# Two transformer blocks on one core: whole x tiles first, a narrower wait at the second gated group, six projection groups by column blocks

## The reference, cut to what matters

```python
h = rmsnorm(x, norm_mix_g)
proj = h @ w_in            # 1024 x 15368
(ml_q, ml_k, ml_v, ml_o, ml_i, ml_f, sc_b, sc_c, sc_u,
 sb_q, sb_k, sb_v, g_ml, g_sc, g_sb) = split(proj)
y_ml = head_rmsnorm(sigmoid(ml_o) * mlstm(ml_q, ml_k, ml_v, ml_i + b_i, ml_f + b_f))
y_sc = short_conv(sc_b, sc_c, sc_u, conv_w)
y_sb = stick_breaking(sb_q, sb_k, sb_v)      # 16 heads of 64
merged = sigmoid(g_ml)*(y_ml @ w_ml_proj) + sigmoid(g_sc)*(y_sc @ w_sc_proj) + sigmoid(g_sb)*(y_sb @ w_sb_proj)
x = x + merged @ w_out
x = x + square(relu(rmsnorm(x) @ w_up)) @ w_down
x = rmsnorm(x, norm_final_g)
# second block
x = x + rms_norm(hybrid_mixer(rms_norm(x), ...) @ w_out_2)
h = rms_norm(x, pre_ffn_norm)
x = x + rms_norm((silu(h @ w_ffn_gate) * (h @ w_ffn_up)) @ w_ffn_down)
```

## Time and profile before

| | us |
|---|---|
| median of the timed runs (919.97, 922.23, 922.33) | 922.23 |
| the profiled execution's own time | 922.42 |
| its span in the trace | 920.7 |
| TensorE busy | 907.2 |
| VectorE busy | 591.8 |
| ScalarE busy | 489.7 |
| GpSimd busy | 45.4 |

### The profile page before, as it was taken

One profiled execution on the slowest core, in us unless ns is written; L12 is line 12 of the kernel. 1 busy time (PEld: TensorE's weight loads), 2 busy tenths in 40 slices (PEclk: granted clock), 3 DMA queues, 4 the chain that ended last, 5 costly groups with the idle time before them and its releaser, 6 DMA issues. The chain is left out here.

```text
span 920.7 us, 12881 instructions
## 1 busy us (share of the span) xinstructions
PE 907.2 (99%) x5334; PEld 791.6 (86%) x5334; DVE 591.8 (64%) x614; ACT 489.7 (53%) x573; POOL 45.4 (5%) x80
## 2 busy tenths in 40 slices
PE   8999999999999999999999999999999989999997
PEld 7998998789998888888888888889987878888886
DVE  4765656567887445556677755557795767777643
ACT  6434877883435443345555543446777755555441
POOL 3010111110010000000000000001000100000000
PEclk9999999999999999999999999999999999999999
DMA  7766444544255555555565565544832475555541
GB/s 251 235 245 227 157 142 136 181 137 132 98 184 183 186 196 205 191 190 201 179 185 186 191 207 194 183 140 144 277 136 92 139 227 184 183 183 206 203 163 46
DMA packets 99818, 163.93 MB, mean 178 GB/s; under 512 B 4896, under 2 KB 37507, under 8 KB 99632
## 3 DMA queue, kind: packets, MB, share of 16 engines
q1 hardware_dynamic: 99760, 163.11, 53.8%
HBM read 162.03 MB, written 3.16 MB: 179 GB/s over the span
## 5 line engine op out<-in xcount | busy, mean ns | idle before, releaser
L1504 DVE TENSOR_TENSOR wlo<-land,whi 128x2048 fp32r<-128x2048 f32 (+2 forms) x152 | 335.1, 2208 | 176.8 <-ACT whi L1077 175.8
L1077 ACT ACTIVATE whi<-land 128x2048 fp32r<-128x2048 f32 (+1 forms) x152 | 280.4, 1848 | 206.8 <-PE acc L546 145.5
L552 PE MATMUL acc<-xT,whi 128*128 128x256 f32 x528 | 152.1, 288 | 0.0
L554 PE MATMUL acc<-xT,whi 128*128 128x256 f32 x528 | 149.3, 283 | 0.0
L556 PE MATMUL acc<-xT,wlo 128*128 128x256 f32 x528 | 149.3, 283 | 0.0
L552 PEld LDWEIGHTS acc<-xT,whi 128*128 128x128 f32 x528 | 101.1, 192 | 2.9 <-issue 2.1
L554 PEld LDWEIGHTS acc<-xT,whi 128*128 128x128 f32 x528 | 101.2, 192 | 0.2
L556 PEld LDWEIGHTS acc<-xT,wlo 128*128 128x128 f32 x528 | 101.2, 192 | 0.0
L544 PE MATMUL acc<-whi,xT 128*128 128x512 f32 (+2 forms) x240 | 91.5, 381 | 0.0
L545 PE MATMUL acc<-wlo,xT 128*128 128x512 f32 (+2 forms) x240 | 90.3, 376 | 0.0
L546 PE MATMUL acc<-whi,xT 128*128 128x512 f32 (+2 forms) x240 | 90.1, 375 | 0.0
(11 more groups left out here) (401 smaller groups left out, 1374.5 us busy)
## 6 DMA issues: line engine op xcount, KB each, us to landing
land<-in_w_in SPq DMA_DIRECT2D x55, 1024.0 KB, 5.1
land<-in_w_up SPq DMA_DIRECT2D x16, 1024.0 KB, 5.3
land<-in_w_down SPq DMA_DIRECT2D x16, 1024.0 KB, 5.1
land<-in_w_ffn_gate SPq DMA_DIRECT2D x22, 512.0 KB, 4.0
land<-in_w_ffn_up SPq DMA_DIRECT2D x22, 512.0 KB, 5.1
land<-in_w_ffn_down SPq DMA_DIRECT2D x10, 1024.0 KB, 5.0
land<-in_w_in SPq DMA_DIRECT2D x14, 512.0 KB, 4.6
land<-in_w_out SPq DMA_DIRECT2D x6, 1024.0 KB, 5.1
```

Source lines behind the costliest of these rows:

```text
L552: mm(to, whi[:, s, k, cs], xh[:, k0 + k, :], start=first and c % 2 == 0, stop=False, skip_group_check=True)
L554: mm(to, whi[:, s, k, cs], xl[:, k0 + k, :], start=False, stop=False, skip_group_check=True)
L1077: activate(whi[:, u % PARTS, 0:m, 0:w], land[:, u % LANDS, 0:m, 0:w], ACT.Copy).then_inc(hi_ready, 1)
L1504: v.tensor_tensor(wlo[:, u % PARTS, 0:m, 0:w], land[:, u % LANDS, 0:m, 0:w], whi[:, u % PARTS, 0:m, 0:w].bitcast(F32), ALU.subtract).then_ ...
```

## The change

Three things. At the **front**, x comes as two whole token tiles, with one tile `lead` between them that holds the identity, the vectors already turned into columns, and the gate biases; the transpose of the vectors and its copy are gone, x is turned tile by tile, seven and four warm matmuls stand where nine and six did, ScalarE's table is loaded by a dummy instruction, the squares of x are taken after unit 2's split, and the spread of the norm's row moves from between units 1 and 2 into unit 2. The **second gated group** waits, ahead of its second pair of banks, for `gate2_ready` and `rest_out` in place of gu0's `read_dve`, and the first and the second pair each do their wlo matmuls right behind their whi matmuls (the same goes for up0). **Six groups** (sbk, mlq, mlk, two each) are done by blocks of 128 output columns: for each block four 512-column matmuls and four 256-column ones into a bank of its own, all four banks by one group; VectorE folds each bank with a reduction (`take_chunk`) and scales afterwards in SBUF. `SIDE` replaces `n % 2`: a group behind one by blocks starts on the same side.

```diff
+SIDE = [0]
+for _n in range(1, len(GROUPS)):
+    SIDE.append(SIDE[-1] if chunked(GROUPS[_n - 1][0]) else 1 - SIDE[-1])
...
     @block.sync
     def _(sp):
-        sp.dma_start(rows[0:V_ROWS, :], dram["vectors"]).then_inc(rows_in, 16)
-        sp.dma_start(con[:, 0:P], dram["con"][:, 0:P]).then_inc(con_in, 16)
...
+        for t in range(TT):
+            sp.dma_start(x_tok[:, t, :], dram["x"][t * P:(t + 1) * P, :]).then_inc(x_in[t], 16)
+            if t == 0:
+                sp.dma_start(lead[:, :], dram["lead"]).then_inc(lead_in, 16)
...
+        def chunk_product(u):
+            n, k0, m = UNITS[u]
+            name, _, _, kk, act, _ = GROUPS[n]
+            s = u % PARTS
+            wait_operand(name, act, k0 + m)
+            for c in range(NG // P):
+                to, cs = acc[:, (SIDE[n] + c // 2) % 2, c % 2, :], slice(c * P, (c + 1) * P)
+                if k0 == 0 and chunked(GROUPS[n - 1][0]):
+                    pe.wait_ge(chunk_read, chunks_before(GROUPS[n - 1][0]) + c + 1)
+                elif k0 == 0 and c == 0 and n >= 2:
+                    group_read(n - 2)
+                elif k0 == 0 and c == 2:
+                    group_read(n - 1)
+                if c == 0:
+                    pe.wait_ge(hi_ready, u + 1)
+                for k in range(m):
+                    mm(to, whi[:, s, k, cs], xT[:, k0 + k].rearrange("p a t -> p (a t)"), start=k0 + k == 0, stop=False,
+                       skip_group_check=True)
+                if c == 0:
+                    pe.wait_ge(lo_ready, u + 1)
+                for k in range(m):
+                    last = mm(to[:, 0:T], wlo[:, s, k, cs], xT_hi[:, k0 + k, :], start=False, stop=k0 + k == kk - 1,
+                              skip_group_check=True)
+                if u == LAST_U[name] and c < NG // P - 1:
+                    last.then_inc(chunk_done, 1)
+            last.then_inc(units_done, 1)
...
+            if k0 == 0 and n >= 1 and chunked(GROUPS[n - 1][0]):
+                pe.wait_ge(chunk_read, chunks_before(GROUPS[n - 1][0]) + 2)
+            elif k0 == 0 and n >= 2:
+                group_read(n - 2)
...
                 if pair is not pairs[0]:
-                    group_read(n - 1)
+                    if name == "gu1":
+                        pe.wait_ge(gate2_ready, 1)
+                        pe.wait_ge(rest_out, D_FF // NG + 1)
+                    else:
+                        group_read(n - 1)
...
-            pe.wait_ge(lo_ready, u + 1)
-            for k in range(m):
-                for c in range(NG // P):
-                    last = mm(to[:, c, 0:T], wlo[:, s, k, c * P:(c + 1) * P], xT_hi[:, k0 + k, :], start=False,
-                              stop=k0 + k == kk - 1, skip_group_check=True)
+                pe.wait_ge(lo_ready, u + 1)
+                for k in range(m):
+                    for c in pair:
+                        last = mm(to[:, c, 0:T], wlo[:, s, k, c * P:(c + 1) * P], xT_hi[:, k0 + k, :], start=False,
+                                  stop=k0 + k == kk - 1, skip_group_check=True)
...
-            if (u, k) == (1, UK):
+            if (u, k) == (2, 2):
                 pe.wait_ge(ones_in, 16)
                 spread(0, "x")
...
+        def take_chunk(name, c):
+            n, j = G_AT[name], int(name[3])
+            if c < 3:
+                dve.wait_ge(chunk_done, 3 * CHUNKED.index(name) + c + 1)
+            else:
+                product_done(name)
+            k = 4 * j + c
+            to = {"sbk": sbkT, "mlq": mlqT, "mlk": mlkT}[name[:3]][:, k, :]
+            v.tensor_reduce(to, acc[:, (SIDE[n] + c // 2) % 2, c % 2, :].rearrange("p (a t) -> p t a", a=2), AX.X,
+                            ALU.add).then_inc(chunk_read, 1)
...
+            if ends and chunked(name):
+                for c in (0, 1):
+                    take_chunk(name, c)
...
-                product_done(name)
-                v.scalar_tensor_tensor(out=to[:, 4 * j:4 * j + 4, :], in0=flat.rearrange("p (a b) -> p a b", b=T),
+                to = to[:, 4 * j:4 * j + 4, :]
+                if chunked(name):
+                    chunks_taken(name)
+                else:
+                    product_done(name)
+                v.scalar_tensor_tensor(out=to, in0=to if chunked(name) else flat.rearrange("p (a b) -> p a b", b=T),
```

More of the change, by code:

```diff
@@ L152, in whole, with chunked, chunks_before @@
     return name[:2] == "up" or name[:2] == "gu" and name != "gu0"
+def chunked(name):
+    return name[:3] in ("sbk", "mlq", "mlk")
+CHUNKED = [grp[0] for grp in GROUPS if chunked(grp[0])]
+SIDE = [0]
+for _n in range(1, len(GROUPS)):
+    SIDE.append(SIDE[-1] if chunked(GROUPS[_n - 1][0]) else 1 - SIDE[-1])
+def chunks_before(name):
+    return 4 * CHUNKED.index(name)
 def reads_before(n, eng):
@@ L198, in build @@
     con = sb("con", [P, K_END], side="right")
+    lead = sb("lead", [P, L_END], side="right")
     diag = sb("diag", [P, TT, P], side="right")
-    rows = diag[:, 0, :]
     row = sb("row", [P, T], side="right")
-    vecs = sb("vecs", [P, V_ROWS], side="right")
     squares = sb("squares", [P, 7, 2, TT], side="right")
@@ L921, in warm, with first_turn @@
             for _ in range(times):
[L922 removed]
+                mm(acc[:, 1, 1, :], ymlT_hi[:, 0, 0:P], ymlT_hi[:, 0:2, :].rearrange("p a b -> p (a b)"), start=True,
                    stop=True)
[L925 to L933 removed]
+        def first_turn():
+            for t in range(TT):
+                pe.wait_ge(x_in[t], 16)
+                for k in range(KD):
+                    last = nc.tensor.transpose(M[k // 2][:, (k % 2 * TT + t) * P:(k % 2 * TT + t + 1) * P],
+                                               x_tok[:, t, k * P:(k + 1) * P], ident)
+                    if t == TT - 1 and k % 2 == 1:
+                        last.then_inc(turned, 1)
+                if t == 0:
+                    warm(4)
+        pe.wait_ge(heat_set, 1)
+        warm(7)
+        pe.wait_ge(lead_in, 16)
+        first_turn()
         def between(u, k):
@@ L1888, in _ @@
                 last.then_inc(if_lo, 1)
+            if u == 0:
+                make_diag(0, 0)
             if u == LAST_U["psc1"]:
@@ L2024, in _ @@
                 if name[:3] == "out":
-                    last = v.tensor_tensor(x, acc[:, n % 2], x, ALU.add)
+                    last = v.tensor_tensor(x, acc[:, SIDE[n]], x, ALU.add)
                 else:
```

168 lines of the change are left out of this document (82 added, 86 removed).

## The result

The changed kernel takes 915.45 us (median of four runs, 915.28 to 915.87), the kernel before 921.87 (four runs, 919.97 to 922.33). The ratio is 0.9933, 95% interval 0.9921 to 0.9944: a gain of 6.4 us (0.7%), clear of the noise, where 6.8 was forecast against the profiled execution. The profiled execution of the changed kernel took 915.87 us with a span of 914.2, against 922.42 and 920.7.

What follows compares the result with a forecast made beforehand. TensorE, busy 907.2 of 920.7 us, was taken as the bound. Terms of -4.2 (gu1), -0.3 (blocks) and -2.3 (front) sum to -6.8 against 922.42: 915.6, rounded to 915.7; 8-in-10 range 913.0 to 918.9.

Steps and rivals of the forecast that it cites:

- The sum: Whole kernel: gu1, blocks and front together save 6.8 us against the profiled execution's 922.42, giving 915.6, rounded to 915.7.
- gu1, -4.2: Second gated group: 4.2 us saved, 1.4 by earlier release, 1.0 by work pulled ahead, 1.8 by the clock.
- The one for the clock: Second gated group: eight matmuls after the wait take 1.82 us instead of 3.50 at full clock, saving 1.8.
- release alone, clock falls anyway: Bound for the second gated group: only the earlier release counts, pulled work is hidden, -1.4 us.
- Blocks, -0.3: Groups sbk, mlq, mlk: merged matmuls save 2.4 us, stalls cost 1.5 at four handovers and 0.6 at sbv0.
- Front, -2.3: Before unit 2: it starts at 22.6 instead of 25.35, 2.75 us sooner; the moved spread leaves -2.3 net.
- (a): Six groups by blocks: VectorE's reductions are hidden in its idle time; -8.9 us, 913.5; chance 0.13.
- (b): Front gives nothing: weights land at 10, clock rises late, first 16 blocks run slow; -4.5 us, 917.9; chance 0.15.
- (c): gu1: clock still falls after the 0.4 us wait; -5.0, 917.4, or with only the release -4.0, 918.4; chance 0.10.
- (d): Five block handovers: VectorE becomes the bound; reductions at 1.3 us cost 6.5, at 1.7 give 924 or above; chance 0.04.
- (e): gu1 still waits because its first unit's wlo, needed after eight matmuls, is late; 919.8; chance 0.03.

Runs made afterwards that it cites:

- gu_wait_only: Changed kernel with the new wait in gu1 kept but its wlo matmuls behind both pairs again, the old order: 916.32 us.
- front_only: Changed kernel with the six groups' blocks undone and gu1's old wait and order restored, so only the new front stays: 918.79 us.
- fill: Kernel before, with eleven unread 512-column matmuls put ahead of gu1's second pair to feed TensorE during its wait: 920.86 us.
- rest_first: Changed kernel with VectorE's sbw_lo pair ahead of the unit's split at four handovers: 914.69 us, and 913.98 us when repeated.
- x_after_half: Changed kernel with the second token tile of x asked for behind the first half tile of weights: 916.05 us.
- double: Changed kernel with the third and fourth reduction of each group by blocks done twice on VectorE: 918.65 us.

## Why the prediction was right, point by point

- **The sum** was -6.8 (915.6); measured -6.4 between medians, -6.5 between profiled spans. The three terms were -4.2, -0.3 and -2.3; the marks give -3.9, -0.3 (with +0.46 for the spread taken out) and -2.3. That the total came so close is luck in part: it compares with an execution in which the clock fell in gu1, one of the longer group of 34 among 41 runs; against the shorter group the gain is 4.6, and the start of unit 2 alone varies by 1.4 us.
- **gu1, -4.2.** The mechanism held step for step: the release by the product on VectorE, with a wait of 0.4 as forecast (0.24 in the row, 0.40 by the distances between starts), the pulled work worth its own length (0.94 in `gu_wait_only`), and no fall of the clock behind the short wait. Its terms were 1.4, 1.0 and 1.8 and came out at 1.40, 0.94 and 1.56. The one for the clock was too large: the 4.2 is a difference from 749.39, read off the chain, while the other times are of the timeline, where the next unit starts at 749.23 (0.16), and the first unit now takes 6.09 us and not the 5.97 added up, since the restart behind the wait costs 0.1. Nor do the eight matmuls carry the whole price of the fall: from start to start they take 3.31 us before and 1.95 in `front_only`, the sixteen narrow ones behind them 2.13 and 1.91. That no fall was counted for the short wait rested on one row, the wait of 1.93 at the front with full rate behind it; `fill` shows the same wait with the clock at 0.50 behind it. So this premise was weak, and the conclusion right: 1.00 behind 0.24 in the seven profiled executions with the new wait and the new order, and behind 1.2 in `gu_wait_only`. The bound "release alone, clock falls anyway" was never met. What the step didn't foresee is that the clock term isn't always there to be won: in `front_only` the old wait brings no fall, and the same edit would have given 2.3.
- **Blocks, -0.3.** The total is right because two sizes were wrong in opposite directions. The saving was put at 0.20 a unit from rows of the up groups; a block unit takes 5.61 and gains 0.14 by `rest_first` (12 x 0.14 = 1.7, not 2.4). The rule of the Trainium skill weighed there (page "TensorE: Matmul & The Clock Gate", section "Wait — 56ns, not 53.3ns?") gave 0.5, by about 2.5 ns for each merged pair; measured, a pair gives 9 ns (1.7 us over 192), so the rule falls further short than the rows overshoot. The price was put at 1.5 at the four handovers (0.5, 0.2, 0.5, 0.3) and 0.6 at sbv0; it was 1.2 (0.1, 0.35, 0.15, 0.5 and 0.1 behind the last: they do alternate, but the other way round) and about 0.2 (12 x 0.14 less 1.2 less the 0.3 that is left; by the stretches, 0.56 - 0.45 + 0.10). At sbv0 three things were each a little better than forecast: VectorE's split began at 55.58, which in the time of the kernel before (2.28 later) is 57.86 and not 58.05; two reductions take 1.24 and not 1.36; and the four units ahead save 0.56 and not 0.78, so that TensorE comes 0.22 later. That is 0.53 of the 0.6; the restart adds 0.1. A reduction was put at 0.68, by a row with 4 partitions; with 128 it takes 0.62 to 0.64, so the time goes by columns, as assumed.
- **Front, -2.3.** Forecast: first half tile at 9.2, first weight matmul near 10, unit 2 at 22.6. Traced: 9.24, 9.98, 22.64. The closeness is partly luck: over eleven executions of kernels with this front unit 2 started between 21.55 and 22.99, and in two with the old front at 25.38 and 26.30. The price of the spread, 0.45, was 0.46. VectorE's chain ends where it was put (its half of wlo is done at 11.85), but TensorE has only just come to it (11.99), so that from 9.98 on the matmuls themselves are as much the bound as VectorE.
- **Rivals.** (a), reductions hidden: not so, but `rest_first` shows what it would have been worth, 1.2 us of the 2.1 that it claimed. (b), a slow first unit: not here, as the warm matmuls at 6.20 and the sixteen at 9.98 (2.17 us) show, nor in any of the twelve profiled executions with the new loading. The price it names is real, but on the old front: in `fill` the sixteen took 3.65. The rise of the clock can be late: in `x_after_half` (first row of the fence there) the same four take 1.61, and it cost nothing, since TensorE then waited for x anyway. (c), the clock falls after the short wait: it stayed at 1.00 each time. (d), VectorE as the bound: `double` makes it so and still ends at 918.65, as stalls alternate; at 1.3 us for each of the two reductions behind the softplus pair, 3.35 us of the gain go (2.37 and 0.98), not 6.5 as (d) claimed. (e): gu1's first pair didn't wait for its wlo, which VectorE made from 734.14 on, both units in 4.49 us.

## What to carry to other kernels

Ask of every wait which instruction reads the buffer last, and wait for that one; a counter raised at the end of a chain of three operations keeps the buffer for all three. Then put work that needs neither buffer ahead of what is left of the wait: it counts in full as long as the wait is longer than the work (0.94 of 0.96 here). Where an edit adds work on a second engine, look at what stands behind it that the first engine waits for, and move that ahead of what has slack: here the pair that TensorE waited for stood behind a split that had none waiting, and exchanging the two was worth 1.2 us more.

## What the hardware showed that was not expected

- **A wait of 2.6 us on TensorE costs 2.6 or 4.2.** Behind the same unfilled wait the granted clock fell to 0.50 (1.2 GHz) in four of five profiled executions and stayed at 1.00 in the fifth; a fall costs 1.6 us more. At the old front a wait of 1.93 us did the same in one of two. A single profile doesn't tell which one an average run sees; the mean granted clock of the timed runs (0.999 against 0.995 to 0.997 in the kernel before) tells more.
- **Merging matmuls gives what the pattern around them allows.** A 512-column matmul and its 256-column partner take 0.228 and 0.119 us in rows of sixteen (3.65 and 1.91), together 0.347; in blocks of four and four 0.351 (5.61 for sixteen pairs). That is 0.05 us per unit, a quarter of what the merge was expected to bring.
- **Short stalls don't show.** The waits list 0.2 us for `sbw_lo` once, where `rest_first` shows 1.2 us at four handovers. The ends of matmuls in a profile are modelled (the last of a row of 256-column ones is shown 0.28 us long where the next could start after 0.12), so a gap shorter than this tail vanishes. Distances between starts show it.
